# Remainders of the last pair of each gate-up group made by an adding DMA in a two-block fp32 kernel

## The chip, the cores and the metric

The kernel runs on one core of one Trainium2 chip. The metric is the device time of one execution in microseconds, the median of several runs; lower is better.

## The reference

Two transformer blocks run one after the other on 256 tokens of width 2048, all in float32. The change touches only the feed-forward part of the second block, which is

```
y = _rms(h, norm_ffn_g[i])
h = h + (jax.nn.silu(y @ w_gate[i]) * (y @ w_up[i])) @ w_down[i]
```

with `w_gate` and `w_up` of 2048 x 5632 and `w_down` of 5632 x 2048.

## The kernel before, in words

Every weight matrix is read once. A *unit* is one weight tile of 128 x 2048 (1 MB, four blocks of 512 columns). The 370 units are worked in a fixed order that `plan` writes out; each engine's program loops over the same list, and semaphores that only count up tie the engines together. Precision is kept by splitting: a weight tile `raw` becomes a rounded part `hi` (fp32r, a copy on ScalarE, line 1068) and a remainder `lo = raw - hi` (VectorE, line 1497, written in place of `raw`). The tokens are split likewise (XH, XL), and each product is three matmuls in `three` (lines 564 to 566): hi by hi, hi by lo, lo by hi.

The gate-up stage is 11 groups ("ff", 0) to ("ff", 10) of eight units each, kind "pair": units 218 to 337, with groups of `w_down` between some of them. A pair unit holds two blocks of gate and two of up. Five of the eight units ("others") take 24 matmuls of 128 x 512; three ("seven", the set `g.seven`) take 21, by a seven-product scheme that needs VectorE to form sums of weights first (`weight_sums`, lines 1517 to 1523) in a second tile (`t_slot`, `th_slot`), which ScalarE then rounds in line 1072.

In a group the seven-product units are the first, third and fifth (in group 0 the third, fifth and seventh). After the last of them comes the *crossing*: ScalarE copies bank P1 of PSUM to E (`begin_sums`, line 1322, which waits for that unit to be done), and VectorE adds the banks P6, P7 and P5 in four operations (`cross`, lines 1542 to 1545), counted by `crossed_over`. After the last unit, `finals` (lines 1551 and 1553) adds the other banks; then follow the tanh (`gate_tanh`) and the product (`hide`, lines 1558 and 1560). TensorE later transposes that product (`flip`, line 794), in `side(u)` for the seventh unit of the *next* group (`TURNH`). The transposes write bank pair psB[:, 0], which are the banks P1 and P6 of the running group, so they wait until `crossed_over` has counted that group's crossing:

```
if u in TURNH:
    j = TURNH[u]
    e.wait_ge(hb_made, j + 1)
    e.wait_ge(flip_low, HIDDEN + j)
    if j < 10:
        e.wait_ge(crossed_over, j + 2)
```

The order on ScalarE around this is, for each u: `side(u)`, then `splits(u)` (the splits of all units whose `position` is u), then `begin_sums` if u is the last seven-product unit. On VectorE it is `side`, `weight_sums`, `hide`, `split`, the end of `weight_sums`, `cross`, and `finals` or `post`.

Buffers are handed out ahead of time by the class `Places`: each unit takes the place used longest ago, and the writer waits until the unit that last used it is done. In the gate-up stage there are five places for `hi` and seven for `raw`/`lo`. Weight loads are issued by SyncE in unit order, each when its `raw` place is free (lines 494 and 495 for a pair). GpSimd issues only a few small loads (`gpsimd_program`).

`position(u)` is u - 2 for a pair unit and u - 3 for others: ScalarE and VectorE split unit u when their loops are at that index.

Of the kernel before, what the change touches and what calls it, by code (L numbers as in the profile page):

```python
# [11 lines left out]
ALU = mybir.AluOpType  # L12
# [142 lines left out]
def build_hybrid(nc, A, C, out, scratch):  # L155
    with ExitStack() as ctx:
        def sem(name):
            return ctx.enter_context(nc.semaphore(name))
# [101 lines left out]
        with ExitStack() as p5:  # L260
# [40 lines left out]
        x_landed = [sem(f"x_landed{i}") for i in range(4)]  # L301
        id_landed, vr_landed, rb_landed, oh_landed, fc_landed = [sem(n + "_landed") for n in ("id", "vr", "rb", "oh", "fc")]
        rb_filled, zeros_made, squares_made, rx_made = sem("rb_filled"), sem("zeros_made"), sem("squares_made"), sem("rx_made")
# [18 lines left out]
        srd_made, sb_dotted, sb_made = sem("srd_made"), sem("sb_dotted"), sem("sb_made")  # L322
        ln_landed, bs_landed, pw_landed, sw_landed = [sem(n + "_landed") for n in ("ln", "bs", "pw", "sw")]
        sw_turned, sw_made = sem("sw_turned"), sem("sw_made")
# [13 lines left out]
        xf_made, xs_summed, xs_high, xs_low, weights_summed = [sem(n) for n in (  # L338
            "xf_made", "xs_summed", "xs_high", "xs_low", "weights_summed")]
        e0_made, crossed_over, left_done, finals_made, hb_made = [sem(n) for n in (  # L340
            "e0_made", "crossed_over", "left_done", "finals_made", "hb_made")]
# [11 lines left out]
        l_slot, l_before, h_slot, h_before = [], [], [], []  # L353
        t_slot, t_before, th_slot, th_before = {}, {}, {}, {}
        landed, total_landed = [], [0] * R_FFN
        hi_after, lo_after, hi_count, lo_count = [], [], 0, 0
        summed = {}
        for u, (g, _) in enumerate(units):
            extended = ffn[0] <= u <= ffn[1]
            for slots, befores, places in ((l_slot, l_before, l_places), (h_slot, h_before, h_places)):  # L360
                slot, before = places.take(u, extended)
                slots.append(slot)
                befores.append(before)
            if u in g.seven:
                t_slot[u], t_before[u] = l_places.take(u, extended)
                th_slot[u], th_before[u] = h_places.take(u, extended)
                summed[u] = len(summed)
            twice = g.kind in ("narrow", "pair") or not isinstance(g.cols, (int, type(None)))
            total_landed[l_slot[u]] += 0 if u < 2 else 32 if twice else 16
            landed.append(total_landed[l_slot[u]])  # L370
            hi_count += 1 + (u in g.seven)
            lo_count += 1 + (u in g.seven)
            hi_after.append(hi_count)
            lo_after.append(lo_count)

        def position(u):

            return u - 2 if units[u][0].kind == "pair" else u - AHEAD

# [135 lines left out]
        def gpsimd_program(e):  # L515
            e.wait_ge(unit_done, 1)
            for dst, src in ((VR[0:16, :], vec("norm_w")), (VR[16:32, :], vec("norm_mix_g_2")),
                             (VR[32:48, :], vec("norm_ffn_g_2")), (VR[48:64, :], vec("norm_ple_g_2")),
                             (VR[64:68, :], vec("cf_conv_b_2")), (VR[68:72, :], vec("cf_ln_g_2")),
                             (VR[72:76, :], vec("cf_ln_b_2")), (VR[76:80, :], vec("pool_scale_2")),  # L520
                             (VR[80:81, :], A["diff_subln_w"]),
                             (VR[81:93, :], A["sc_conv_w_2"].rearrange("a j (r c) -> (a j r) c", c=128)),
                             (CR[:, :], A["cf_conv_w_2"].rearrange("a j (r c) -> (a j r) c", c=128)),
                             (TR[:, :], C["c_tr"])):
                e.dma_start(dst, src).then_inc(vr_landed, 16)
            e.wait_ge(rb_filled, 1)
            e.dma_start(RB[0:32, :], A["rel_bias"]).then_inc(rb_landed, 16)
            for dst, src in ((OH[0:33, :, :], C["c_oh"]), (CM[:, :], C["c_cm"]), (FB, rows(A["fox_b_f"], 4)),
                             (LQ[:, 0:64], rows(A["diff_lq1"], 64)), (LQ[:, 64:128], rows(A["diff_lk1"], 64)),
                             (LQ[:, 128:192], rows(A["diff_lq2"], 64)), (LQ[:, 192:256], rows(A["diff_lk2"], 64))):  # L530
                e.dma_start(dst, src).then_inc(oh_landed, 16)
            e.dma_start(FC, C["c_fc"]).then_inc(fc_landed, 16)

            e.wait_ge(bias_made, 1)
            e.dma_start(scratch[0:8, :], G[0:8, 0, :]).then_inc(bias_out, 16)
            e.dma_start(scratch[8:12, :], G[0:4, 1, :]).then_inc(bias_out, 16)
            e.wait_ge(bias_out, 32)
            e.dma_start(BT[:, :, :], bass.AP(scratch.tensor, scratch.offset, [[1, 128], [384, 12], [1, 256]])).then_inc(bt_landed, 16)

            e.wait_ge(flip_turned, MERGED + 4)  # L540
            for f in range(4):
                e.dma_start(cols(f), xv[:, :, 512 * f:512 * f + 512]).then_inc(xr_landed[f], 16)
                if f == 0:
                    e.dma_start(FW[:, :], rows(A["final_norm_w"], 2048)).then_inc(fw_landed, 16)

            e.wait_ge(unit_done, done(("out", 3)))
            e.wait_ge(srd_made, 1)
            e.dma_start(LG[:, 0, :], rows(A["sgu_ln_g_2"], 512)).then_inc(ln_landed, 16)
            e.dma_start(LG[:, 1, :], rows(A["sgu_ln_b_2"], 512)).then_inc(ln_landed, 16)
            e.dma_start(BS[:, :], rows(A["sgu_b_2"], 512)).then_inc(bs_landed, 16)  # L550
            e.dma_start(PW[:, :, :], A["pool_w_2"][0].rearrange("g c d -> c g d")).then_inc(pw_landed, 16)
            e.dma_start(B[:, 1, 0:512].rearrange("p (h s) -> p h s", h=4),
                        A["sgu_w_2"][0].rearrange("h t s -> t h s")).then_inc(sw_landed, 16)

            e.wait_ge(unit_done, done(("down", 7)))
            e.dma_start(PP[:, :, :], A["p_2"][0, 0].rearrange("(t p) c -> p t c", p=128)).then_inc(p_landed, 16)

            e.wait_ge(unit_done, done(("down", 11)))
            e.dma_start(FG[:, :], rows(A["final_norm_g_2"], 2048)).then_inc(fg_landed, 16)


        def tensor_program(e):
# [96 lines left out]
            def pair_unit(u):  # L659
# [23 lines left out]
                ended.update({p: g.last for p in ("P2", "P3", "P4", "P8")})  # L683
                H1, L1 = hi[h_slot[u]], lo[l_slot[u]]

# [127 lines left out]
            def biases():  # L813
                e.wait_ge(rb_landed, 16)
                e.wait_ge(oh_landed, 7 * 16)
                e.wait_ge(rx_copied, 1)
                e.matmul(psB[0:8, 0, 0:384], RB[:, 0:8], OH[0:33, 0, :], start=True, stop=True)
                e.matmul(psB[0:4, 0, 512:896], RB[:, 8:12], OH[0:33, 1, :], start=True, stop=True).then_inc(bias_dotted, 1)
# [232 lines left out]
        def scalar_program(e):  # L1051
# [8 lines left out]
            def split(u):  # L1060
# [5 lines left out]
                if h_before[u] >= 0:  # L1066
                    e.wait_ge(unit_done, h_before[u] + 1)
                e.activation(hi[h_slot[u]][:, m], raw[l_slot[u]][:, m], ACT.Copy).then_inc(hi_made, 1)  # L1068
                if u in g.seven:
# [387 lines left out]
        def vector_program(e):  # L1457
# [157 lines left out]
            def lambda_dots():  # L1615
                q4 = LQ.rearrange("p (c x d) -> p c x d", c=2, x=2)
                w = LB[:, 0, 0:128].rearrange("p (c d) -> p c d", c=2)
                e.wait_ge(oh_landed, 7 * 16)
                e.wait_ge(bias_dotted, 1)
# [171 lines left out]
            def pool_means():  # L1791
                w4 = c4(B[:, 3, :])
                finish(e.tensor_tensor(P1[:, 2:4, 16:272], P2[:, 2:4, 16:272], P2[:, 2:4, 12:268], ALU.add))
                finish(e.tensor_tensor(P2[:, 3, 16:272], P1[:, 3, 16:272], P1[:, 3, 8:264], ALU.add))
                e.wait_ge(fc_landed, 16)
                e.wait_ge(mix_high, 1)
# [6 lines left out]
            def side(u):  # L1803
# [11 lines left out]
                if u == 12:  # L1815
                    e.wait_ge(wi_made, 1)
                    e.wait_ge(oh_landed, 7 * 16)
                    for t in range(2):
# [68 lines left out]
                if u == 190:  # L1887
                    e.wait_ge(sgu_norm, 1)
                    e.wait_ge(ln_landed, 32)
                    finish(e.tensor_tensor(z2, z2, over(LG[:, 0, :], 2), ALU.mult))  # L1890
                    e.tensor_tensor(z2, z2, over(LG[:, 1, :], 2), ALU.add).then_inc(sgu_v_made, 1)
# [76 lines left out]
            def post(g):  # L1968
# [48 lines left out]
                elif name == "scc":  # L2017
                    gelu_end(B[:, 3, :], B[:, 2, :], 2)
                    ps, t4 = [x.rearrange("p (h t s) -> p h t s", h=4, t=2) for x in (psB[:, 1, :], B[:, 2, :])]
                    e.wait_ge(spatial_dotted, 1)  # L2020
                    e.wait_ge(bs_landed, 16)
                    e.tensor_tensor(t4[:, :, 0, :], ps[:, :, 0, :], c4(BS[:, :]), ALU.add)
# [47 lines left out]
            for u in range(n_units):  # L2070
# [5 lines left out]
                for v in split_at.get(u, ()):  # L2076
                    split(v)
                if u in sums_at:
# [103 lines left out]
```

## Time and profile before

| | |
|---|---|
| median of 3 runs | 2096.84 us (2096.63 to 2097.2) |
| profiled execution, its own time | 2096.8 us |
| its span | 2094.9 us |
| TensorE busy | 2078.9 us, 99% |
| VectorE busy | 1402.4 us, 67% |
| ScalarE busy | 956.5 us, 46% |
| GpSimd busy | 21.1 us, 1% |
| DMA queue q1 (weights) | 387.64 MB, 54.7% of 16 engines |
| granted TensorE clock | 0.999 |

Engines are PE (TensorE matmul), PEld (its weight load), DVE (VectorE), ACT (ScalarE), POOL (GpSimd) and SP (SyncE); L1068 is line 1068. Times in the timeline are microseconds from the start of the span. The gate-up stage and the `w_down` groups inside it lie between about 1275 and 1920 us.

### The profile page before, as it was taken

The numbers are of one execution on the slowest core, as the hardware profiler recorded it, in microseconds if no ns is written. First come the engines' busy times: TensorE is split into PE (matmuls) and PEld (weight loads), VectorE is DVE, ScalarE is ACT, GpSimd is POOL, SyncE is SP. The second block draws the span as 40 slices with busy tenths as digits, with TensorE's granted clock in tenths as the row PEclk, the third lists the DMA queues.
The fourth block names the chain that finished last, engine by engine and source line by source line (L and its number), as shares of the span: only waits on it lengthen the run. The fifth ranks groups of instructions, "written<-read, shape, count | busy, mean of one in ns | idle before, by whom it ended". The sixth has DMA issues, their size and how long they took to land.

```text
span 2094.9 us, 25122 instructions
## 1 busy us (share of the span) xinstructions
PE 2078.9 (99%) x10496; PEld 1768.9 (84%) x10496; DVE 1402.4 (67%) x1427; ACT 956.5 (46%) x914; POOL 21.1 (1%) x40
## 2 busy tenths in 40 slices
PE   9999999999999999999999999999999999999998
PEld 8888888888888888888999988788888888888887
DVE  5576555665544455455789858999658986587565
ACT  5544443544343434444444455555435544355443
POOL 2000000000000000000000000000000000000000
PEclk9999999999999999999999999999999999999999
DMA  8655455454555555575655564556645566455553
GB/s 248 217 177 180 162 168 193 161 181 169 193 189 193 196 187 198 183 253 189 203 185 164 178 220 161 186 200 219 220 152 199 199 217 218 149 205 188 187 202 120
DMA packets 226144, 398.38 MB, mean 190 GB/s; under 512 B 12610, under 2 KB 57914, under 8 KB 225776
## 3 DMA queue, kind: packets, MB, share of 16 engines
q1 hardware_dynamic: 222752, 387.64, 54.7%
q0 software_dynamic: 2528, 8.00, 1.3%
q8 instruction: 84, 1.38, 0.3%
q10 hardware_dynamic: 752, 1.12, 0.1%
q14 instruction: 28, 0.23, 0.0%
HBM read 394.62 MB, written 2.12 MB: 189 GB/s over the span
## 4 chain that ended last, share of the span: by engine, by line
PE 91%; DVE 6%; ACT 1%; issue 1%; DMA 1%; ACTq 0%; SPq 0%; DVEq 0%
PE psA L564 23%; PE psA L566 23%; PE psA L565 23%; PE psA L737 6%; PE psA L741 3%; PE psB L564 3%; PE psB L565 3%; PE psB L566 3%; DVE lo L1497 2%; DVE CA L1765 1%; PE psB L794 1%; ACT hi L1068 0%; DVE raw L1521 0%; ACT hi L1072 0%; DMA X<-in_x_dram 0%
## 5 line engine op out<-in xcount | busy, mean ns | idle before, releaser
L1497 DVE TENSOR_TENSOR lo<-raw,hi 128x2048 fp32r<-128x2048 f32 (+3 forms) x401 | 889.1, 2228 | 400.7 <-ACT hi L1068 394.9
L1068 ACT ACTIVATE hi<-raw 128x2048 fp32r<-128x2048 f32 (+3 forms) x368 | 679.6, 1859 | 485.9 <-PE psA L566 355.2
L564 PE MATMUL psA<-hi,XHL 128*128 128x512 f32 (+1 forms) x1434 | 560.9, 391 | 1.6 <-DVE E L1551 1.6
L566 PE MATMUL psA<-hi,XHL 128*128 128x512 f32 (+1 forms) x1434 | 556.8, 388 | 0.0
L565 PE MATMUL psA<-lo,XHL 128*128 128x512 f32 (+1 forms) x1434 | 556.4, 388 | 0.0
L564 PEld LDWEIGHTS psA<-hi,XHL 128*128 128x128 f32 x1434 | 269.4, 188 | 56.8 <-DVE E L1551 2.0
L566 PEld LDWEIGHTS psA<-hi,XHL 128*128 128x128 f32 x1434 | 269.2, 188 | 55.8
L565 PEld LDWEIGHTS psA<-lo,XHL 128*128 128x128 f32 x1434 | 269.5, 188 | 53.9
L564 PE MATMUL psA<-hi,YH 128*128 128x512 f32 x488 | 190.6, 391 | 0.0
L566 PE MATMUL psA<-hi,YL 128*128 128x512 f32 x488 | 189.9, 389 | 0.0
L565 PE MATMUL psA<-lo,YH 128*128 128x512 f32 x488 | 189.9, 389 | 0.0
L564 PE MATMUL psA<-XHL,hi 128*128 128x256 f32 (+1 forms) x528 | 150.4, 285 | 0.5 <-DVE lo L1601 0.5
L565 PE MATMUL psA<-XHL,hi 128*128 128x256 f32 (+1 forms) x528 | 149.5, 283 | 0.0
L566 PE MATMUL psA<-XHL,lo 128*128 128x256 f32 (+1 forms) x528 | 149.4, 283 | 0.0
L737 PE MATMUL psA<-XHL,hi 128*128 128x512 f32 x576 | 138.6, 393 | 0.0
L737 PEld LDWEIGHTS psA<-XHL,hi 128*128 128x128 f32 x576 | 106.0, 188 | 21.5 <-issue 0.6
L566 PEld LDWEIGHTS psA<-hi,YL 128*128 128x128 f32 x488 | 91.6, 188 | 19.1
L564 PEld LDWEIGHTS psA<-hi,YH 128*128 128x128 f32 x488 | 91.6, 188 | 18.7
L565 PEld LDWEIGHTS psA<-lo,YH 128*128 128x128 f32 x488 | 91.6, 188 | 18.7
L1072 ACT ACTIVATE hi<-raw 128x2048 fp32r<-128x2048 f32 x33 | 63.2, 1916 | 93.8 <-DVE raw L1517 83.7
L564 PEld LDWEIGHTS psA<-XHL,hi 128*128 128x128 f32 (+1 forms) x528 | 100.8, 191 | 1.0 <-DVE XHL L1608 0.8
L565 PEld LDWEIGHTS psA<-XHL,hi 128*128 128x128 f32 (+1 forms) x528 | 100.8, 191 | 0.2
(385 smaller groups left out, 2030.0 us busy)
## 6 DMA issues: line engine op xcount, KB each, us to landing
raw<-in_w_in_dram SPq DMA_DIRECT2D x158, 1024.0 KB, 4.9
raw<-in_w_gate_dram SPq DMA_DIRECT2D x88, 512.0 KB, 3.8
raw<-in_w_up_dram SPq DMA_DIRECT2D x88, 512.0 KB, 4.7
raw<-in_w_down_dram SPq DMA_DIRECT2D x44, 1024.0 KB, 5.1
raw<-in_w_out_dram SPq DMA_DIRECT2D x32, 1024.0 KB, 5.1
raw<-in_w_branch_dram SPq DMA_DIRECT2D x16, 1024.0 KB, 5.1
raw<-in_w_ple_gate_dram SPq DMA_DIRECT2D x16, 1024.0 KB, 5.1
raw<-in_w_in_dram SPq DMA_DIRECT2D x16, 512.0 KB, 4.7
```

What stands on the lines that cost most here:

```text
L564: e.matmul(dst, A2[0], B2[0], start=first, stop=False, skip_group_check=True)
L565: e.matmul(dst, A2[0], B2[1], start=False, stop=False, skip_group_check=True)
L566: return e.matmul(dst, A2[1], B2[0], start=False, stop=last, skip_group_check=True)
L737: e.matmul(both, hh[:, s], XHL[:, kb, :, :].rearrange("p a t -> p (a t)"), start=i == 0 and n < 2, stop=False, skip_group_check=True)
L741: x = e.matmul(both[:, 256:512], ll[:, s], XH[:, kb, :], start=False, stop=i == len(g.parts) - 1 and n >= 14, skip_group_check=True)
L794: x = e.transpose(ps[:, k, 128 * t:128 * t + 128], src(t, k), ID[:, :])
L1068: e.activation(hi[h_slot[u]][:, m], raw[l_slot[u]][:, m], ACT.Copy).then_inc(hi_made, 1)
L1072: e.activation(hi[th_slot[u]][:, :], raw[t_slot[u]][:, :], ACT.Copy).then_inc(hi_made, 1)
L1497: e.tensor_tensor(lo[l][:, m], raw[l][:, m], hi[h][:, m].bitcast(F32), ALU.subtract).then_inc(lo_made, 1)
L1765: x = e.scalar_tensor_tensor(out=CA[:, c, :], in0=HP[:, c, j:j + 256], scalar=CW[:, 4 * j + c:4 * j + c + 1], in1=CA[:, c, :], op0=ALU.mul ...
```

## The change

For the last unit u of each gate-up group, VectorE no longer makes the remainder. That unit takes a second `hi` place, `n_slot[u]`. ScalarE writes the negated rounded weights there before it writes `hi` itself. A DMA issued by GpSimd then adds `raw` to that place, so it ends as `raw - hi`; TensorE uses it as the remainder. The position of this unit on ScalarE moves from u - 2 to u - 3. Three semaphores are merged into others to free two.

```
             if g.kind == "pair" and u == g.last:
+                n_slot[u], n_before[u] = h_places.take(u, extended)
...
-            lo_count += 1 + (u in g.seven)
+            lo_count += 1 + (u in g.seven) - (u in n_slot)
...
-            return u - 2 if units[u][0].kind == "pair" else u - AHEAD
+            return u - 2 if units[u][0].kind == "pair" and u not in n_slot else u - AHEAD
...  gpsimd_program
+            def remainders(first, last):
+                for j in range(first, last + 1):
+                    u = named[("ff", j)].last
+                    e.wait_ge(negated, j + 1)
+                    e.dma_start(hi[n_slot[u]][:, :], raw[l_slot[u]][:, :], accum_op=ALU.add).then_inc(lo_landed, 16)
+            remainders(0, 8)
             e.wait_ge(unit_done, done(("down", 7)))
             e.dma_start(PP[:, :, :], ...).then_inc(p_landed, 16)
+            remainders(9, 10)
...  pair_unit (TensorE)
-                H1, L1 = hi[h_slot[u]], lo[l_slot[u]]
+                H1, L1 = hi[h_slot[u]], hi[n_slot[u]] if u in n_slot else lo[l_slot[u]]
+                if u in n_slot:
+                    e.wait_ge(hi_made, hi_after[u])
+                    e.wait_ge(lo_landed, 16 * j + 16)
...  split (ScalarE)
                 if h_before[u] >= 0:
                     e.wait_ge(unit_done, h_before[u] + 1)
+                if u in n_slot:
+                    e.wait_ge(unit_done, n_before[u] + 1)
+                    e.activation(hi[n_slot[u]][:, m], raw[l_slot[u]][:, m], ACT.Copy, scale=-1.0).then_inc(negated, 1)
                 e.activation(hi[h_slot[u]][:, m], raw[l_slot[u]][:, m], ACT.Copy).then_inc(hi_made, 1)
...  VectorE's loop
                 for v in split_at.get(u, ()):
-                    split(v)
+                    if v not in n_slot:
+                        split(v)
```

The rest of the diff is the merging of `fc_landed` into `oh_landed` and of `bs_landed` into `ln_landed`, with the waits' counts raised to match.

## Rows read from the trace of the kernel before

**Rows 1.** The page: busy time, and the chain that ended last by engine and line.
```profile
PE 2078.9 (99%) x10496; PEld 1768.9 (84%) x10496; DVE 1402.4 (67%) x1427; ACT 956.5 (46%) x914; POOL 21.1 (1%) x40
...
PE 91%; DVE 6%; ACT 1%; issue 1%; DMA 1%; ACTq 0%; SPq 0%; DVEq 0%
PE psA L564 23%; PE psA L566 23%; PE psA L565 23%; PE psA L737 6%; PE psA L741 3%; PE psB L564 3%; PE psB L565 3%; PE psB L566 3%; DVE lo L1497 2%; DVE CA L1765 1%; PE psB L794 1%; ACT hi L1068 0%; DVE raw L1521 0%; ACT hi L1072 0%; DMA X<-in_x_dram 0%
```

**Rows 2.** Waits in 1290 to 1930 us: who for whom, total us, times, longest.
```profile
ACT E L1322 <- PE psA L566: 65.2, 11, 6.4
...
PE psA L564 <- DVE E L1551: 1.6, 1, 1.6
...
PE psB L794 <- DVE THF L1560: 1.1, 1, 1.1
```

**Rows 3.** Windows view of that stretch: us, busy PE, PEld, DVE, ACT, POOL, clock, DMA.
```profile
1290.00:1930.00 640.00, 637.26 (x2856) 528.03 (x2855) 502.00 (x366) 304.63 (x202) 0.71 (x1) 1.00 0.57 197
```

**Rows 4.** Timeline of group 2's crossing: start us, duration us, engine, line, operands.
```profile
1384.59 0.37 SPq L494 DMA_DIRECT2D raw<-in_w_gate_dram  x1
1384.59 0.60 ACT L1322 ACTIVATE E<-psB 128x512 f32<-128x512 f32 x1 [6.42 <-PE psA L566]
...
1387.27 0.68 DVE L1545 TENSOR_TENSOR E<-E,psB 128x512 f32<-128x512 f32 x1
...
1389.73 2.29 DVE L1497 TENSOR_TENSOR lo<-raw,hi 128x2048 fp32r<-128x2048 f32 x1
1389.84 1.04 PE L794 MATMUL psB<-ID,THF 128*128 128x128 f32 x8
...
1396.20 0.39 PE L564 MATMUL psA<-hi,XHL 128*128 128x512 f32 x1
```

**Rows 5.** The same two instructions in groups 1 and 10, first and last of ten.
```profile
1342.22 0.60 ACT L1322 ACTIVATE E<-psB 128x512 f32<-128x512 f32 x1 [6.41 <-PE psA L566]
...
1347.46 1.03 PE L794 MATMUL psB<-ID,THF 128*128 128x128 f32 x8
...
1897.79 0.60 ACT L1322 ACTIVATE E<-psB 128x512 f32<-128x512 f32 x1 [6.42 <-PE psA L566]
...
1903.04 1.04 PE L794 MATMUL psB<-ID,THF 128*128 128x128 f32 x8
```

**Rows 6.** Timeline of ScalarE alone: copies back to back.
```profile
1350.84 1.91 ACT L1072 ACTIVATE hi<-raw 128x2048 fp32r<-128x2048 f32 x1
...
1352.64 3.28 ACT L1068 ACTIVATE hi<-raw 128x2048 fp32r<-128x2048 f32 x2
...
1374.45 3.72 ACT L1068 ACTIVATE hi<-raw 128x2048 fp32r<-128x2048 f32 x2 [1.79 <-PE psA L566]
```

**Rows 7.** Timelines of ScalarE, VectorE and TensorE around the end of group 0.
```profile
1299.58 3.29 ACT L1068 ACTIVATE hi<-raw 128x2048 fp32r<-128x2048 f32 x2
1306.70 1.92 ACT L1072 ACTIVATE hi<-raw 128x2048 fp32r<-128x2048 f32 x1 [3.83 <-DVE raw L1517]
1309.71 0.60 ACT L1322 ACTIVATE E<-psB 128x512 f32<-128x512 f32 x1 [1.09 <-PE psA L566]
...
1308.65 2.29 DVE L1497 TENSOR_TENSOR lo<-raw,hi 128x2048 fp32r<-128x2048 f32 x1 [0.20 <-ACT hi L1072]
...
1319.44 0.50 PE L564 MATMUL psA<-hi,XHL 128*128 128x512 f32 x1 [1.61 <-DVE E L1551]
```

**Rows 8.** Landing of GpSimd's 1 MB load of FG, and of the X loads.
```profile
FG<-in_final_norm_g_dram POOLq DMA_DIRECT2D x1, 1024.0 KB, 7.2
...
DMA to landing us min/median/max: 7.5/11.7/13.8
```

**Rows 9.** GpSimd's queue in 2000.9 to 2001.9 us: packets, MB, share of 16 engines.
```profile
q0 software_dynamic: 50, 0.41, 96.6%
```

**Rows 10.** Windows view after group 2's crossing; DMA share and GB/s are last.
```profile
1390.00:1392.00 2.00, 2.00 (x15) 1.79 (x13) 2.00 (x2) 1.09 (x2) 0.00 (x0) 1.00 0.77 291
...
1394.00:1396.00 2.00, 2.00 (x11) 1.65 (x10) 2.00 (x2) 2.00 (x2) 0.00 (x0) 1.00 0.00 0
```

More of the change, by code:

```diff
@@ L301, in build_hybrid @@
         x_landed = [sem(f"x_landed{i}") for i in range(4)]
-        id_landed, vr_landed, rb_landed, oh_landed, fc_landed = [sem(n + "_landed") for n in ("id", "vr", "rb", "oh", "fc")]
+        id_landed, vr_landed, rb_landed, oh_landed = [sem(n + "_landed") for n in ("id", "vr", "rb", "oh")]
         rb_filled, zeros_made, squares_made, rx_made = sem("rb_filled"), sem("zeros_made"), sem("squares_made"), sem("rx_made")
@@ L322, in build_hybrid @@
         srd_made, sb_dotted, sb_made = sem("srd_made"), sem("sb_dotted"), sem("sb_made")
-        ln_landed, bs_landed, pw_landed, sw_landed = [sem(n + "_landed") for n in ("ln", "bs", "pw", "sw")]
+        ln_landed, pw_landed, sw_landed = [sem(n + "_landed") for n in ("ln", "pw", "sw")]
         sw_turned, sw_made = sem("sw_turned"), sem("sw_made")
@@ L339, in build_hybrid @@
             "xf_made", "xs_summed", "xs_high", "xs_low", "weights_summed")]
+        negated, lo_landed = sem("negated"), sem("lo_landed")
         e0_made, crossed_over, left_done, finals_made, hb_made = [sem(n) for n in (
@@ L353, in build_hybrid @@
         l_slot, l_before, h_slot, h_before = [], [], [], []
-        t_slot, t_before, th_slot, th_before = {}, {}, {}, {}
+        t_slot, t_before, th_slot, th_before, n_slot, n_before = {}, {}, {}, {}, {}, {}
         landed, total_landed = [], [0] * R_FFN
@@ L363, in build_hybrid @@
                 befores.append(before)
+            if g.kind == "pair" and u == g.last:
+                n_slot[u], n_before[u] = h_places.take(u, extended)
             if u in g.seven:
@@ L531, in gpsimd_program @@
                 e.dma_start(dst, src).then_inc(oh_landed, 16)
-            e.dma_start(FC, C["c_fc"]).then_inc(fc_landed, 16)
+            e.dma_start(FC, C["c_fc"]).then_inc(oh_landed, 16)
             e.wait_ge(bias_made, 1)
@@ L549, in gpsimd_program @@
             e.dma_start(LG[:, 1, :], rows(A["sgu_ln_b_2"], 512)).then_inc(ln_landed, 16)
-            e.dma_start(BS[:, :], rows(A["sgu_b_2"], 512)).then_inc(bs_landed, 16)
+            e.dma_start(BS[:, :], rows(A["sgu_b_2"], 512)).then_inc(ln_landed, 16)
             e.dma_start(PW[:, :, :], A["pool_w_2"][0].rearrange("g c d -> c g d")).then_inc(pw_landed, 16)
@@ L814, in biases @@
                 e.wait_ge(rb_landed, 16)
-                e.wait_ge(oh_landed, 7 * 16)
+                e.wait_ge(oh_landed, 8 * 16)
                 e.wait_ge(rx_copied, 1)
@@ L1617, in lambda_dots @@
                 w = LB[:, 0, 0:128].rearrange("p (c d) -> p c d", c=2)
-                e.wait_ge(oh_landed, 7 * 16)
+                e.wait_ge(oh_landed, 8 * 16)
                 e.wait_ge(bias_dotted, 1)
@@ L1794, in pool_means @@
                 finish(e.tensor_tensor(P2[:, 3, 16:272], P1[:, 3, 16:272], P1[:, 3, 8:264], ALU.add))
-                e.wait_ge(fc_landed, 16)
+                e.wait_ge(oh_landed, 8 * 16)
                 e.wait_ge(mix_high, 1)
@@ L1816, in side @@
                     e.wait_ge(wi_made, 1)
-                    e.wait_ge(oh_landed, 7 * 16)
+                    e.wait_ge(oh_landed, 8 * 16)
                     for t in range(2):
@@ L1888, in side @@
                     e.wait_ge(sgu_norm, 1)
-                    e.wait_ge(ln_landed, 32)
+                    e.wait_ge(ln_landed, 48)
                     finish(e.tensor_tensor(z2, z2, over(LG[:, 0, :], 2), ALU.mult))
@@ L2020, in post @@
                     e.wait_ge(spatial_dotted, 1)
-                    e.wait_ge(bs_landed, 16)
+                    e.wait_ge(ln_landed, 48)
                     e.tensor_tensor(t4[:, :, 0, :], ps[:, :, 0, :], c4(BS[:, :]), ALU.add)
```

## The prediction

> **What bounds the kernel now.** I read the page's busy times first, then the waits and the windows of the gate-up stage, then the timeline of one group. TensorE is busy 2078.9 of 2094.9 us, and the chain that ended last is TensorE for 91% [rows 1]. Between 1290 and 1930 us it is busy 637.26 of 640 us, at full clock, with VectorE at 502 us and ScalarE at 305 us [rows 3]; all its waits there are one of 1.6 us and one of 1.1 us [rows 2]. So an engine that is relieved here can give back 2.7 us at most. What the change can do is to make something late for TensorE.
>
> The tightest place in a group is the crossing. In group 2 ScalarE sits idle 6.42 us until the last seven-product unit (u = 238) is done, copies P1 to E at 1384.59, and VectorE ends its fourth addition at 1387.27 + 0.68 = 1387.95. The transposes that must wait for `crossed_over` start at 1389.84 [rows 4], so they start unblocked with 1.9 us in hand. From the start of E's copy to the transposes is 5.25 us, in group 1 5.24 and in group 10 5.25 [rows 5]; the eight groups between repeat it. Ten groups have such transposes; in group 0 the seventh unit has none.
>
> **What the change removes.** Eleven remainders of 2.29 us on VectorE [rows 4], 25 us. I count them as 0 for the end: TensorE had no wait that they caused, except perhaps the 1.6 us one. A chain may name VectorE for 6% because it is followed back through the engine that was last, but in this stretch the waits are 2.7 us in all.
>
> **What it adds on ScalarE.** The last unit of group 2 is 241. Its position was 239, after the crossing; now it is 238, and at one index ScalarE runs `splits` before `begin_sums`. So both its copies, the negated and the plain one, now stand ahead of E's copy. Could they run early, in the 6.42 us of idleness? No: handing out the five `hi` places by the rule of `Places`, the new place of unit u was last used by u - 3, that is by 238 itself, in all eleven groups. The negation waits for the very event for which E's copy waits. It starts at 1384.59, and E's copy follows two full copies later. Two back to back take 3.72 us from start to end [rows 6]; starts follow each other by 1.80 (1350.84 to 1352.64, rows 6), so E's copy is late by 3.6 to 3.7 us. I take 3.65. I cost a copy with a factor of -1 as a plain one of 1.91 us; the trace has no such form over a whole tile. At half of that the stall would be 0.95 us shorter, at twice 1.9 us longer, in each of ten groups (-9.5 and +19 us).
>
> Behind E's copy wait the four additions, and behind them the transposes: 1387.95 + 3.65 = 1391.60 against 1389.84, 1.76 us of stall, and about 0.1 us for TensorE to start again from idle (its first matmul after the 1.6 us wait shows 0.50 us where others show 0.39, rows 7 and 4). That is 1.85 us in each of ten groups, **18.5 us**. VectorE is not late beyond this: its next work (sums for the third unit of the next group, flip remainder, split of the next first unit) comes 3.65 us later but without the 2.29 us remainder, so 1.4 us later, and TensorE itself is 1.85 us later.
>
> Group 0 has another order. Its second places shift too: the second `hi` place of unit 226 (first of group 1) was last used by 223 and now by 224. Its copy ran at 1306.70; now it waits for unit 224, whose end shows as the start of E's copy, 1309.71 [rows 7]. It is 3.0 us late, and after it come E's copy, the remainder of 226 (1308.65, rows 7), the additions and `finals`, for which TensorE already waited until 1319.44 [rows 7]. These are in series on VectorE, so the whole **3.0 us** reach TensorE. In the other groups the first unit's second place is last used by u - 3, early enough.
>
> Sum: 18.5 + 3.0 = 21.5 us.
>
> **What it adds on GpSimd and the DMA.** Issue is no matter: the queue is otherwise empty here, and the P and FG loads stand behind remainders that are long due. What matters is landing. The negation ends at 1384.59 + 1.91 = 1386.5; with 0.1 us to wake GpSimd the DMA is issued at 1386.6. Unit 241 starts at 1396.20 in the trace [rows 4], and at 1398.05 after the 1.85 us stall. So a landing time L up to 9.6 us costs nothing in any case, up to 11.45 us nothing beyond the 21.5, and from there each microsecond costs one in each of ten groups. No DMA that adds is in the trace. The nearest row is GpSimd's 1 MB load of FG, L = 7.2 us; the far end is 13.8 us, the slowest of the four X loads issued together with FW [rows 8]. FG's data moved at 0.41 MB per us on 96.6% of the engines [rows 9], so 2.6 us of its 7.2 are data and 4.6 are start and finish. Weight loads in the way: those issued from 1384.59 (rows 4) are over soon after 1391, and at 1394 to 1396 the engines carry nothing [rows 10], so the adding DMA meets a mostly free stretch. I take L between 7.2 and 11, hidden. At 13.8 it would cost 2.35 us in each of ten groups above the sum, 23.5 us; in group 0 the negation would follow at 1299.58 and the DMA be issued near 1301.6, landing at 1315.4, while unit 225 starts as 224 ends, about 1309.5 [rows 7]; of these 5.9 us group 0's own 3.0 us cover half, and 2.9 are left. That end is 48 us in all.
>
> The Trainium skill, Collectives: The Full Stack (Part 3, "The bandwidth ceiling"), says that a DMA that adds is slower because it needs two source reads, and so runs at about half the rate of a copy. No run so far shows it. By that rule FG's 2.6 us of data would be an estimated 5.2 us and L about 9.8 us, plus up to 1 us of shared engines, still under 11.45; the sum stays, but the reserve would shrink to under 2 us, which is why the rival of a late DMA has the second largest chance.
>
> **The rivals.**
> *The DMA is late.* L above 11.45, because adding reads the place and writes it back, 8 KB row after row. For it: nothing in the trace adds, and the reserve over FG is only 4.25 us. Against it: the quiet stretch. Time: the stalls are not added but the larger counts, L - 9.6 per group. L = 13.8 gives +48 (2145); L = 17 gives 7.4 us in ten groups and 9 in group 0, +83 (2180).
> *The stall is absorbed, no change.* This holds if the delay of E's copy is under the 1.9 us in hand, that is if only one copy stood ahead of it (1.8 us). The code puts two there, both behind the same event; only a negation much faster than 1.91 us would do. Time: +3 from group 0 or 0, 2097 to 2100.
> *Faster.* One mechanism: the eleven remainders are in truth what paces TensorE in the stage, through a lock-step in which it waits less than the profile resolves; the chain does name lo L1497 for 2% [rows 1]. It decides as soon as VectorE's lead counts and not ScalarE's. Price 11 x 2.2 = 24 us, 2073. Against it stand 637.26 of 640 us.
>
> **How the numbers follow.** The sum is made against the profiled execution, 2094.9 us of span and 2096.8 us of time; the median of the runs is 2096.84, the same to 0.1. So the forecast is 2096.8 + 21.5 = 2118.3 us. Chances: this forecast (2109 to 2125) 0.65; late DMA 0.25; absorbed 0.06; faster 0.02; the rest in smaller stalls. The low end, 2109, is the sum with a negation at half the time; the high end, 2146, is the far bound of L. A change within 0.2% (4.2 us) is about what a measurement of this kernel can't tell from none: faster 0.02, same 0.07, slower 0.91.
>
> **What would show it.** In the profile after, the waits view should have a row of TensorE line 794 waiting for the additions of `cross` (L1545), ten times, near 1.8 us each; E's copy should start 3.65 us after the SyncE loads that the same unit releases, with two copies ahead of it. TensorE's wait for the E additions in group 1 should grow from 1.6 us by 3.0 (in one piece or two). The adding DMA should land in under 11.4 us, and TensorE should have no wait for it. The prediction is wrong in its size if that wait appears, with L from the issues view, and wrong in its mechanism if the transposes don't wait, or if E's copy starts where it did.

## The result, and the profile after

The kernel after takes **2130.45 us** in the median (2129.47 to 2131.89), the kernel before 2096.88 us (2096.63 to 2097.2) beside it. The ratio is 1.0161, with a 95% interval of 1.0149 to 1.0174: slower by 33.6 us. The forecast was 2118.3 us. The direction holds and the time lies within the outer bounds of 2109 to 2146 us, but outside the bracket of 2109 to 2125 us that had a chance of 0.65; the size is 12 us short. The profiled run of after took 2131.89 us with a span of 2130.1 us, 35.2 us more than the span before; the accounts below are made against these 35.2.

The page of after, busy time, chain and GpSimd's queue, answers to [rows 1]:

```profile
PE 2084.9 (98%) x10496; PEld 1767.8 (83%) x10496; DVE 1380.1 (65%) x1416; ACT 976.6 (46%) x925; POOL 30.6 (1%) x51
...
q0 software_dynamic: 4112, 19.54, 3.8%
...
PE 86%; DVE 5%; DMA 5%; ACT 2%; issue 1%; ACTq 0%; SPq 0%; DVEq 0%
```

The instruction counts say that the change is what it claims: eleven fewer on VectorE (22 us less busy), eleven more on ScalarE (20 us more), eleven more on GpSimd. (Of the semaphores two are merged into others, those of FC and BS, not three.) In the chain TensorE falls from 91% to 86%, and DMA, which had 1%, now has 5%. Where TensorE stands still is in its waits view from 1290 to 1975 us (who for whom, total us, times, longest), to be laid beside [rows 2]:

```profile
PE psB L809 <- DVE E L1563: 17.8, 10, 1.8
PE psA L576 <- DMA hi<-raw: 6.1, 10, 1.7
PE psB L809 <- DVE THF L1578: 2.9, 1, 2.9
PE psA L576 <- DVE E L1569: 2.7, 1, 2.7
PE psB L576 <- DVE E L1563: 1.0, 1, 1.0
```

Before, two waits made 2.7 us. The first row is the one forecast. The second was forecast not to be there.

The same crossing as [rows 4], in the timeline of after (start us, duration us, engine, line, operands, idle time before it and what ended that):

```profile
1389.87 0.37 SPq L497 DMA_DIRECT2D raw<-in_w_gate_dram  x1
...
1389.96 1.92 ACT L1085 ACTIVATE hi<-raw 128x2048 fp32r<-128x2048 f32 x1 [6.50 <-PE psA L578]
...
1390.80 0.47 SPq L497 DMA_DIRECT2D raw<-in_w_gate_dram  x1
...
1391.78 1.90 ACT L1086 ACTIVATE hi<-raw 128x2048 fp32r<-128x2048 f32 x1
...
1392.17 0.85 POOL L563 DMA_DIRECT2D hi<-raw  x1 [44.23 <-ACT hi L1085]
...
1393.59 0.57 ACT L1340 ACTIVATE E<-psB 128x512 f32<-128x512 f32 x1
...
1396.24 0.68 DVE L1563 TENSOR_TENSOR E<-E,psB 128x512 f32<-128x512 f32 x1
...
1397.06 1.06 PE L809 MATMUL psB<-ID,THF 128*128 128x128 f32 x8 [1.78 <-DVE E L1563]
...
1404.35 0.47 PE L576 MATMUL psA<-hi,XHL 128*128 128x512 f32 x1 [0.75 <-DMA hi<-raw]
```

Read it in order. ScalarE has again been idle for 6.5 us until TensorE finished the seven-product unit, and then it makes the negated copy, the plain copy, and only after them E's copy, 3.63 us after the unit's end. The additions follow, and the transposes stand for 1.78 us. GpSimd issues the adding DMA at 1392.17, and at the last unit TensorE has waited 0.75 us for it when it starts at 1404.35, 12.2 us after the issue.

The issue view and the tile view of the adding DMA (times, KB each, median us from issue to landing; then its spread):

```profile
hi<-raw POOLq DMA_DIRECT2D x11, 1024.0 KB, 11.8
...
DMA to landing us min/median/max: 6.9/11.8/13.0
```

The lowest, 6.9 us, is the last group, where only the tail of one load, 0.23 MB, was still under way at the issue; group 0 has 8.1; the groups between, where SyncE has just issued two 1 MB loads (each in two halves in the timeline above), have 11.5 to 13.0. The queues in two stretches of group 2 show how (packets, MB, share of the 16 engines). At 1396.2 to 1397.2 us, over 4 us after the issue, SyncE's queue still has the engines and GpSimd's queue has no row. At 1398.2 to 1402.2 us it is the other way round:

```profile
q1 hardware_dynamic: 121, 0.24, 89.2%
...
q0 software_dynamic: 101, 0.83, 99.5%
q1 hardware_dynamic: 28, 0.05, 3.7%
```

One more thing is not in the waits. After group 10 TensorE waits 2.85 us for VectorE's `THF`, and toward the end of this wait a stretch of 6.8 us at half clock (1.2 GHz) begins. Timeline, then windows (us, busy PE, PEld, DVE, ACT, POOL, clock, DMA share, GB/s):

```profile
1959.54 0.69 PE L809 MATMUL psB<-ID,THF 128*128 128x128 f32 x2 [2.85 <-DVE THF L1578]
```

```profile
1950.00:1960.00 10.00, 7.15 (x32) 5.68 (x31) 6.98 (x7) 9.48 (x9) 0.00 (x0) 0.94 1.03 381
1960.00:1970.00 10.00, 10.00 (x38) 8.24 (x37) 7.22 (x4) 4.67 (x4) 0.00 (x0) 0.72 0.13 48
1970.00:1980.00 10.00, 10.00 (x46) 8.29 (x45) 4.71 (x3) 2.88 (x2) 0.00 (x0) 1.00 0.59 211
```

At 1960 to 1970 us TensorE is fully busy, but with 38 matmuls against 46 in the next window, and its clock is 0.72. Busy time alone would not have shown it. Matmul by matmul, the trace of after falls 1.7 us further behind that of before in the wait and 2.8 us more in the stretch.

### The profile page after: what moved, and what is told of

It is laid out like the page before. It is cut to its first block, busy times and chain, and to the rows that moved or that the text cites. A ratio compares the mean times of both kernels' runs of the same rounds, so it can differ in the third digit from the quotient of the medians.

```text
span 2130.1 us, 25144 instructions
## 1 busy us (share of the span) xinstructions
PE 2084.9 (98%) x10496; PEld 1767.8 (83%) x10496; DVE 1380.1 (65%) x1416; ACT 976.6 (46%) x925; POOL 30.6 (1%) x51
## 4 chain that ended last, share of the span: by engine, by line
PE 86%; DVE 5%; DMA 5%; ACT 2%; issue 1%; ACTq 0%; SPq 0%; DVEq 0%
PE psA L576 22%; PE psA L578 22%; PE psA L577 22%; PE psA L752 6%; DMA hi<-raw 5%; PE psA L756 3%; PE psB L576 3%; PE psB L578 3%; PE psB L577 3%; DVE lo L1515 2%; DVE CA L1783 1%; PE psB L809 1%; ACT hi L1085 1%; ACT hi L1086 0%; DMA X<-in_x_dram 0%
## 5 line engine op out<-in xcount | busy, mean ns | idle before, releaser
L1515 DVE TENSOR_TENSOR lo<-raw,hi 128x2048 fp32r<-128x2048 f32 (+2 forms) x390 | 864.9, 2226 | 419.9 <-ACT hi L1086 410.4
L577 PE MATMUL psA<-lo,XHL 128*128 128x512 f32 (+1 forms) x1346 | 522.2, 388 | 0.0
L577 PEld LDWEIGHTS psA<-lo,XHL 128*128 128x128 f32 x1346 | 252.9, 188 | 50.4
L752 PEld LDWEIGHTS psA<-XHL,hi 128*128 128x128 f32 x576 | 105.9, 188 | 21.5 <-issue 0.6
L578 PEld LDWEIGHTS psA<-XHL,lo 128*128 128x128 f32 (+1 forms) x528 | 100.7, 191 | 0.0
## 6 DMA issues: line engine op xcount, KB each, us to landing
hi<-raw POOLq DMA_DIRECT2D x11, 1024.0 KB, 11.8
```

The lines of the kernel that those rows point to most:

```text
L577: e.matmul(dst, A2[0], B2[1], start=False, stop=False, skip_group_check=True)
L578: return e.matmul(dst, A2[1], B2[0], start=False, stop=last, skip_group_check=True)
L752: e.matmul(both, hh[:, s], XHL[:, kb, :, :].rearrange("p a t -> p (a t)"), start=i == 0 and n < 2, stop=False, skip_group_check=True)
L1515: e.tensor_tensor(lo[l][:, m], raw[l][:, m], hi[h][:, m].bitcast(F32), ALU.subtract).then_inc(lo_made, 1)
```

## The experiments

The theory after the result, called A in the expectations, was that two copies ahead of E's copy and the second place of group 0 make 21.5 us, and that the rest is the adding DMA. The rivals, named where they were formed, were that relief of VectorE has a value of its own, that the delays add up, and that the DMA is slow for another reason than adding. All times below are medians, and ratios are against runs of the kernel before beside each. A trace is of one execution, whose time can lie some us off the median.

**VectorE adds in place of the DMA.** The negation and both places stay.

```diff
-                    e.dma_start(hi[n_slot[u]][:, :], raw[l_slot[u]][:, :], accum_op=ALU.add).then_inc(lo_landed, 16)
+                    pass
...  pair_unit (TensorE)
-                    e.wait_ge(lo_landed, 16 * j + 16)
+                    e.wait_ge(lo_landed, j + 1)
...  VectorE's loop, behind the other splits
+                if u + 2 in n_slot:
+                    v = u + 2
+                    e.wait_ge(hi_made, hi_after[v])
+                    n = hi[n_slot[v]][:, :]
+                    e.tensor_tensor(n, raw[l_slot[v]][:, :], n.bitcast(F32), ALU.add).then_inc(lo_landed, 1)
```

> As the changed kernel, but VectorE adds the weights to the negated part (position u - 2, after the crossing) and no DMA is issued. Theory A (two causes: two copies ahead of E's copy, worth 1.95 us in each of ten groups, and a late adding DMA, worth 0.85 us in each; group 0 and the proj units add about 5 us): the ten waits of the transposes stay at 1.8 us each, TensorE waits for no DMA, 2121 to 2123 us. Rival B (what exceeds my 21.5 us comes from the order and the places, not from the DMA): 2130 us.

Measured: 2129.82 us (2129.43 to 2130.47), ratio 1.0159 (1.0143 to 1.0174), the same as after. Its waits of TensorE:

```profile
PE psB L809 <- DVE E L1563: 17.8, 10, 1.8
PE psA L576 <- DVE E L1569: 7.4, 8, 2.7
```

The transposes wait exactly as in after, so that wait is not the DMA's. But the wait for the final additions (L1569), once 2.7 us in after, now comes eight times with 7.4 us: group 0's 2.7 and seven of 0.67. With E's copy late, VectorE's work after the crossing is late too, and 2.29 us of remainder in it reach TensorE by about 1 us in each of seven groups. Relief of VectorE is worth that, but only because the same change made the crossing late. Theory A missed here. The time is the one of rival B, but B's account does not follow from it: the seven waits are those of the addition put in the DMA's place, and the next run, with neither, does not have them and is 5 us faster. B holds at most for what is left there.

**A DMA that copies instead of adding.** The last unit's remainder is then not the difference but the weights themselves.

```diff
-                    e.dma_start(hi[n_slot[u]][:, :], raw[l_slot[u]][:, :], accum_op=ALU.add).then_inc(lo_landed, 16)
+                    e.dma_start(hi[n_slot[u]][:, :], raw[l_slot[u]][:, :]).then_inc(lo_landed, 16)
```

> As the changed kernel, but the DMA copies the weights instead of adding them (the remainder is wrong). Theory A: the adding costs twice the data time (5.0 against 2.6 us), so the landing falls from 11.8 to about 9.3 us, TensorE does not wait for it, 2121 to 2123 us. Rival C (the landing is set by the queueing behind the two weight loads and not by the adding): landing stays above 11 us and the time at 2130 us.

Measured: 2124.53 us (2122.53 to 2125.03), ratio 1.0131 (1.0116 to 1.0146). First its waits, then its landings and one window:

```profile
PE psB L809 <- DVE E L1563: 17.8, 10, 1.8
```

```profile
hi<-raw POOLq DMA_DIRECT2D x11, 1024.0 KB, 8.9
...
DMA to landing us min/median/max: 4.2/8.9/9.6
```

```profile
1320.00:1330.00 10.00, 7.28 (x19) 5.73 (x20) 9.97 (x9) 6.22 (x5) 0.00 (x0) 0.66 0.15 51
```

TensorE has no wait for this DMA. From E's copy of group 1 to that of group 10 it takes 573.36 us, against 581.37 us in after: adding instead of copying costs **8.0 us**. The landing is near theory A's 9.3 us and under rival C's 11; but queueing is a large part of it too. Landing is 4.2 us in the last group and 8.9 us behind loads, where adding takes 6.9 and 11.8. The time is 1.5 us above the expectation. The trace has a stretch of 6.8 us at half clock near 1320 us, in which its matmuls fall 2.8 us behind; that was not in the sum.

**One copy ahead of E's copy, with the adding DMA and with the plain one.** In groups 1 to 10 only the negation stays ahead, and the plain copy follows E's.

```diff
                     e.activation(hi[n_slot[u]][:, m], raw[l_slot[u]][:, m], ACT.Copy, scale=-1.0).then_inc(negated, 1)
+                    if u - 3 in CROSS:
+                        return
...
                     begin_sums(CROSS[u], u)
+                    if u + 3 in n_slot:
+                        v = u + 3
+                        e.activation(hi[h_slot[v]][:, :], raw[l_slot[v]][:, :], ACT.Copy).then_inc(hi_made, 1)
```

> As the changed kernel, but in groups 1 to 10 only the negation stands ahead of E's copy; the plain copy follows it. Theory A (the larger of the two delays counts): E's copy is 1.8 us late against 1.9 us in hand, the transposes do not wait, but TensorE now meets the adding DMA 1.95 us earlier and waits about 2.6 us for it in each group: 2128 to 2131 us. Rival D (the two delays add up): 2096.9 + 33.6 - 19.5 = 2111 us.

> Both edits together: one copy ahead of E's copy, and a DMA that copies instead of adding (the remainder is wrong). Theory A: no wait at the transposes, landing 9.3 us against 9.6 us at hand, so TensorE waits 0 to 0.3 us a group; what is left is group 0 and the proj units: 2101 to 2106 us. Rival D: 2111 - 8 = 2103 us as well, so this run only tells what is left of both. If B holds: 2111 us or more.

Measured: 2133.26 us (2127.64 to 2136.05), ratio 1.0171 (1.0156 to 1.0187), and with the plain DMA 2108.69 us (2108.09 to 2109.18), ratio 1.0057 (1.004 to 1.0074). A wait of the first, then two of the second:

```profile
PE psA L576 <- DMA hi<-raw: 20.3, 10, 3.5
```

```profile
PE psA L576 <- DVE E L1574: 2.7, 1, 2.7
PE psA L576 <- DMA hi<-raw: 2.2, 3, 0.9
```

In neither do the transposes wait: 1.8 us of delay fits into the 1.9 us in hand. The 17.8 us went, and with the adding DMA they came back as its wait, 20.3 us in place of 6.1. So the two delays are not added; the later of the two counts, and TensorE's stall at the transposes had been hiding the DMA. With the plain DMA the gain of the one copy does arrive, 15.8 us. Both medians lie above theory A's ranges, by 2 and by 3 us, and far from rival D's 2111 in the first case. In the second's trace two stretches of 3.4 us at half clock, in which its matmuls fall 2.9 us behind, are what the sum left out. The first one's profiled run took 2127.64 us, the shortest of its four; the other three show lower granted clocks (0.993 to 0.995 against 0.998), so its trace holds less half clock than the median run.

**Both copies behind E's copy.** The whole split of the last unit follows `begin_sums`.

```diff
                 for v in split_at.get(u, ()):
-                    split(v)
+                    if not (u in CROSS and v in n_slot):
+                        split(v)
...
                     begin_sums(CROSS[u], u)
+                    if u + 3 in n_slot:
+                        split(u + 3)
```

> As the changed kernel, but in groups 1 to 10 E's copy goes ahead of both copies of the last unit. Theory A: the transposes do not wait; the negation ends 0.5 us later, so the DMA lands 0.5 us later, and TensorE waits about 3.1 us for it in each of the nine groups with a burst of loads ahead of it: 2131 to 2136 us. Rival D (delays add up): 2111 to 2116 us.

Measured: 2137.66 us (2134.24 to 2141.41), ratio 1.0195 (1.0181 to 1.0209).

```profile
PE psA L576 <- DMA hi<-raw: 23.3, 10, 4.2
```

The DMA is issued later and waited for longer, and the time is 1.7 us above the upper end of theory A's range, which had no half clock in it. The trace has seven stretches of it, six of 3.4 us and one of 6.8 us, 27 us in all at 1.2 GHz. Six begin during or soon after a wait for the DMA and one after the wait for `THF`. Up to half of the 27 us, some 13 us, is lost beside the waits.

**The places alone.** The kernel before, with the second `hi` place of each last unit taken and not used.

```diff
+            if g.kind == "pair" and u == g.last:
+                n_slot[u], n_before[u] = h_places.take(u, extended)
```

> The kernel before, with the second hi place taken for the last unit of each group but not used, so that only the hand-out of places moves. Theory A: group 0's chain is 3.0 us late behind unit 224 (about 2.2 us reach TensorE) and the proj units after group 10 cost 1.8 us: 2100 to 2102 us. Rival: the places cost nothing by themselves, 2096.9 us.

Measured: 2103.75 us (2102.3 to 2104.3), ratio 1.0032 (1.0019 to 1.0044). Waits, and one window:

```profile
PE psB L796 <- DVE THF L1562: 2.8, 1, 2.8
PE psA L566 <- DVE E L1553: 2.7, 1, 2.7
...
PE psB L566 <- DVE E L1547: 1.7, 1, 1.7
```

```profile
1930.00:1940.00 10.00, 7.79 (x32) 6.66 (x32) 9.86 (x7) 6.41 (x5) 0.00 (x0) 0.83 0.41 152
```

The median is 7.0 us above before, the span of the profiled run 6.3 us. Of these 6.3 us group 0 makes 3.0: E's copy of group 10 starts at 1900.79 us, against 1897.79 in [rows 5], as forecast. The rest is behind group 10, where with the shifted places TensorE is late too: the wait for `THF` grows from 1.1 to 2.8 us, 1.7 us, and a stretch of 3.4 us at half clock begins as it ends, in which 1.6 us more are lost. The stretch is why the time lies above theory A's 2102 us.

**No remainders at all.** The kernel before without the eleven; TensorE takes the rounded part in their stead.

```diff
-                H1, L1 = hi[h_slot[u]], lo[l_slot[u]]
+                H1, L1 = hi[h_slot[u]], hi[h_slot[u]] if u == g.last else lo[l_slot[u]]
...
-                    split(v)
+                    if not (units[v][0].kind == "pair" and v == units[v][0].last):
+                        split(v)
```

> The kernel before without the eleven remainders of the last units on VectorE; TensorE takes the rounded part in their place, with as many matmuls (the product is wrong). Theory A: nothing waited for them, 2095 to 2097 us. Rival E (VectorE paces TensorE in the stage): 11 x 2.2 us less, 2073 us.

Measured: 2096.14 us (2095.67 to 2096.79), ratio 0.9998 (0.9989 to 1.0007). The wait of [rows 2] that the remainders might have caused falls from 1.6 us to this:

```profile
PE psA L564 <- DVE E L1553: 1.1, 1, 1.1
```

This is the prize of the change at its best, with nothing put in the place of the work removed: 0.6 us of 25 in the medians, which the interval does not tell from none. The rival that forecast 2073 us is out.

**The position alone.** The kernel before, with the last unit's split one unit earlier.

```diff
-            return u - 2 if units[u][0].kind == "pair" else u - AHEAD
+            return u - 2 if units[u][0].kind == "pair" and u != units[u][0].last else u - AHEAD
```

> The kernel before, with the position of each group's last unit at u - 3 as in the changed kernel, and nothing else. Its plain copy then also stands ahead of E's copy, but its place was last used by u - 4, so it runs in ScalarE's idle time. Theory A: no change, 2096 to 2098 us; what hurts is the wait for unit u - 3 and not the position. Rival H (the position alone makes E's copy late): 1.8 us of delay per group, within the 1.9 us in hand or above it, with a TensorE wait at the transposes, 2098 to 2105 us.

Measured: 2096.71 us (2096.29 to 2097.36), ratio 1.0002 (0.9993 to 1.0011). A copy that stands ahead of E's copy in the program but waits for nothing runs in ScalarE's idle 6.4 us. What costs is the place, last used by unit u - 3, not the position.

**The second queued load held back.** After, with SyncE's second load of the burst in groups 1 to 9 waiting until the adding DMA has landed.

```diff
...  for groups 1 to 9
+            free = [v for v in range(last, n_units) if l_before[v] == last - 3]
+            held[free[-1]] = 16 * j + 16
...  SyncE's loads
                     e.wait_ge(unit_done, l_before[u] + 1)
+                if u in held:
+                    e.wait_ge(lo_landed, held[u])
```

> As the changed kernel, but in groups 1 to 9 the second of the two weight loads that SyncE issues when unit u - 3 is done waits until the adding DMA has landed. Theory A (the DMA stands behind the whole burst of 2 MB): its landing falls by one load's 2.6 us from 11.8 to about 9.3 us, TensorE does not wait for it: 2121 to 2124 us, unless the held load is itself late. Rival F (the DMA's long landing is its own, not the burst's): landing stays at 11 to 12 us, 2130 us.

Measured: 2125.52 us (2124.87 to 2127.88), ratio 1.014 (1.0124 to 1.0155). TensorE's largest wait, and the landings:

```profile
PE psB L818 <- DVE E L1572: 17.8, 10, 1.8
```

```profile
DMA to landing us min/median/max: 6.9/7.6/8.1
```

One load less in front, and the landing falls from 11.8 to 7.6 us, more than the 9.3 expected; TensorE's wait for the DMA shrinks to 0.4 us, once, in group 0, whose load was not held. So what made the landing long is the queue in front of it. The time is 1.5 us above theory A's range; a stretch of 3.4 us at half clock near 1323 us, in which 1.6 us are lost, was not in the sum.

**Both mended: one copy ahead, one load held, and then without group 0's and group 10's DMA.** `one_ahead_hold` joins the two diffs above. `nine_groups` also keeps the remainders of groups 0 and 10 on VectorE:

```diff
-            if g.kind == "pair" and u == g.last:
+            if g.kind == "pair" and u == g.last and 0 < g.name[1] < 10:
...  (the counts of negated and lo_landed are one group lower)
```

> Both remedies on the changed kernel: in groups 1 to 10 only the negation ahead of E's copy, and in groups 1 to 9 the second weight load of the burst waits until the adding DMA has landed. Theory A (the larger of the two delays counts, and each has one cause): no wait at the transposes, the landing near 7.6 us is under the 9.6 us at hand, no wait for the DMA; what is left is what places_only showed, 2102 to 2105 us. Rival G (the held loads or the later plain copy make a new wait for TensorE): 2108 us or more.

> As one_ahead_hold, but only groups 1 to 9 make their last remainder by the DMA; groups 0 and 10 stay as in the kernel before, so the places at group 0's end and at the proj units do not move. Theory A: all causes are gone and nothing is gained in return, 2096 to 2098 us. Rival E (relief of VectorE is worth something once nothing else is late): under 2093 us. Rival G: 2100 us or more.

Measured: 2117.75 us (2116.27 to 2121.49), ratio 1.0105 (1.0091 to 1.0119), and 2110.37 us (2109.31 to 2111.71), ratio 1.0067 (1.0054 to 1.0081). They are 13 to 16 and 12 to 14 us above what was expected. A wait and a row of VectorE's timeline in `nine_groups`:

```profile
PE psA L584 <- DVE E L1582: 11.6, 8, 2.1
```

```profile
1401.83 1.23 DVE L1552 TENSOR_TENSOR raw<-raw 128x1024 f32<-128x1024 f32 x1 [2.23 <-DMA raw<-in_w_up_dram]
```

VectorE needs the held load for the sums of the next group's third unit. It waits 2.23 us for it, and the final additions behind that are late for TensorE: of the eight waits one is group 0's old one of 1.6 us, and seven are new, 10.0 us. The other half of rival G, the later plain copy, is out: `one_ahead_plain` has the same late copy and no held load, and its wait for the final additions is group 0's alone (2.7, 1, above). So the held loads make the new wait, and the load cannot be held until the DMA has landed.

**The load held only until the negation.** `nine_groups` with a shorter hold.

```diff
-                    e.wait_ge(lo_landed, held[u])
+                    e.wait_ge(negated, held[u])
```

> As nine_groups, but the held weight load waits only until the negation is made (the event that also releases the adding DMA), not until the DMA has landed. Theory A with what nine_groups showed (its 11.6 us of TensorE waits come from held loads that land 2.2 us too late for VectorE's sums): the load is issued some 7.5 us earlier than there, the DMA has only one load queued ahead or beside it and lands 7.6 to 10 us after its issue, against 9.6 at hand; TensorE waits 0 to 0.5 us a group, 2097 to 2102 us. Rival I (nine_groups' loss is in the plain copy after E's copy or in the places, not in the held load): unchanged, 2110 us.

Measured: 2134.72 us (2133.26 to 2136.92), ratio 1.0183 (1.017 to 1.0197). Both theories missed, by over 20 us: the landing is 12.3 us, where theory A had 7.6 to 10. Issues, waits and landings:

```profile
1390.45 0.37 SPq L505 DMA_DIRECT2D raw<-in_w_gate_dram  x1
...
1390.68 0.88 POOL L571 DMA_DIRECT2D hi<-raw  x1 [45.77 <-ACT hi L1093]
```

```profile
PE psA L584 <- DMA hi<-raw: 24.8, 9, 3.3
```

```profile
DMA to landing us min/median/max: 11.8/12.3/12.8
```

The held load is issued 0.23 us ahead of GpSimd's DMA (the one before it 2.3 us ahead), and the DMA again lands only after it, 12.3 us from its issue. Beside the 24.8 us of waits the trace has six stretches of 3.4 us at half clock, about 10 us lost. Between a hold that is too short (24.8 us of waits) and one that is too long (11.6 us), no point was tried. Even at the best such a version has 0.6 us to win against the kernel before (`no_remainders`), and none of the twelve runs is faster than it by more than can be measured.

## Why the prediction was right, and where it was short

Point by point, in its own order. Two of its terms, 22.8 of the 35.2 us, came as reasoned. The rest is one term put at nothing and one place not looked at, and both errors go the same way. That the total still lies within the outer bounds is owed to their width, set by the far bound of L, and not to the sum.

*TensorE bounds the stage, and VectorE's relief is worth 0.* Right: 2096.14 us without the remainders. It needs the addition that the relief gets a value, about 1 us in seven of the groups, once the crossing is late; this is why the adding DMA and VectorE's adding come out the same (2130.45 and 2129.82), though by other waits.

*Two copies ahead of E's copy, 3.65 us late, 1.85 us in each of ten groups, 18.5 us.* Right. E's copy is 3.63 us late, the transposes wait 1.78 us ten times, and the step from one E copy to the next is 44.36 us in `plain_copy` against 42.38 before, 1.98 us. That is 19.8 us in ten, 1.3 above the term, because TensorE takes 0.2 us and not 0.1 to start again. The negation takes 1.92 us, the same as a plain copy. That the cause is the place and not the position is shown by `early_position`.

*Group 0, 3.0 us.* Right, shown by `places_only`. The waits came in two pieces, 1.0 and 2.7 us for 1.6.

*L between 7.2 and 11 us, hidden.* **This step failed.** L was 11.8 us in the middle groups, 13.0 at most, and it costs 8.0 us, not 0. The limit of 11.45 us was sound: in group 2 the last unit starts 12.2 us after the issue, 0.75 of them waited, so 11.4 would have been free. What was mis-sized is L. The working saw both weight loads ahead of the DMA and priced them as up to 1 us of shared engines, on the ground that they are over soon after 1391 us. But the DMA is issued in the midst of them, and its data wait until they are over, which is nearly 5 us (11.8 against 6.9 in the last group; 8.9 against 4.2 for the plain copy).

The row that L was built on had such a wait in it. In the kernel before, FG's DMA is issued at 1996.94 us, and at 1998.0 to 2000.5 us the only queue with packets is SyncE's (timeline, then the queue view of that stretch):

```profile
1996.94 0.57 POOL L559 DMA_DIRECT2D FG<-in_final_norm_g_dram  x1 [165.72 <-PE psA L566]
```

```profile
q1 hardware_dynamic: 394, 0.81, 89.4%
```

So the 4.6 us read as start and finish were in part a wait behind a load; the whole 1 MB copy of `plain_copy` lands in 4.2 us in its last group. By the prediction's own test, a wait for the DMA in the profile, it is wrong in its size and not in its mechanism. The rival of the late DMA had the mechanism of the larger of the two delays right, as `one_ahead` shows, with the cause put into the addition alone.

The Trainium skill, Collectives: The Full Stack (Part 3, "The bandwidth ceiling"), says of ReduceScatter that it runs at about half of AllGather's rate, since its add needs two source reads. The trace agrees for this DMA inside one core: nearly alone on the engines its queue moved 0.83 MB in 4 us, 0.21 MB per us, against the 0.41 of [rows 9]. The estimate by it, 9.8 us, was high for a nearly idle queue (6.9 us) and low behind two loads.

*Not foreseen.* The shifted places also reach the product behind group 10: TensorE's wait there is 2.9 us for 1.1, 1.7 us more by the unrounded rows, and in the half-clock stretch that begins in it, 6.8 us long, 2.8 us more are lost.

The account: 19.8 + 3.0 + 8.0 + 1.7 + 2.8 = 35.3 us, against 35.2 between the two spans. Of the 13.8 us by which this account exceeds the forecast's 21.5, the DMA makes 8.0, the end behind group 10 makes 4.5, and the restarts at the transposes 1.3. Why a stretch of half clock comes behind one wait and not behind another is open; no run made one at will. The same wait of 2.85 us behind group 10 stands in nine traces, and six of them have a stretch there.

## What to carry to other kernels

Moving work off an engine that is not waited for wins nothing, so price first what the move puts in front of the engine that is: here a copy that waits for a buffer freed only at the end of the tightest unit. Where a transfer is issued in the midst of loads on another queue, count its landing from the end of the loads, not from its issue, and remember that a stall may be hiding it. A new user of a ring of buffers shifts the last user of every later entry, so look at the first units of the next stage as well.

## What was not expected of the hardware

- GpSimd's DMA hardly shared with SyncE's loads that were already queued. Its 1 MB landed 6.9 us after the issue with only the tail of a load under way, 7.6 us with one load of the burst held back, 11.8 us behind both, and 12.3 us behind two of which the second was issued 0.23 us earlier. Once it ran it had 99.5% of the engines and SyncE's queue 3.7%.
- An adding DMA of 1 MB lands 2.7 us later than a copying one (6.9 against 4.2 us in the last group), and its issue takes GpSimd 0.86 us against 0.53.
- Half clock is not decided by the length of the wait before it alone. After waits of 1.9 us (`crossing_first`, 1634.2 us) and 2.05 us (`one_ahead_hold`) a stretch of 3.4 us began, and after one of 3.4 us (`crossing_first`, 1681.9 us) none did. The wait of 2.85 us behind group 10 had a stretch of 6.8 us in after and of 3.4 us in `vector_adds`, `places_only`, `one_ahead_plain`, `hold_loads` and `crossing_first`, and none in `plain_copy`, `one_ahead` and `one_ahead_hold`. `nine_groups`, whose longest wait is 2.1 us, has none.
